# Sums of a closing layer norm moved into the last product, and filler multiplications on TensorE while it waits

## What is computed

```
def second_block(x, ...):
    h = _layernorm(x, ln_in_g, ln_in_b)                        # m = 0
    for layer in range(DEPTH):                                 # DEPTH = 2
        proj = jnp.einsum('bsd,de->bse', h, w_in[layer])
        ...
        y = jnp.einsum('bse,ed->bsd', jnp.concatenate([ya, yb, yc], axis=-1), w_out[layer])
        h = _layernorm(DEEPNORM_ALPHA * h + y, ln_g[layer], ln_b[layer])   # m = 1, 2
    return h

def _layernorm(t, g, b):
    mu = jnp.mean(tf, -1, keepdims=True)
    var = jnp.mean(jnp.square(tf - mu), -1, keepdims=True)
    out = (tf - mu) * lax.rsqrt(var + LN_EPS) * g + b
```

## Time and profile before

| | value |
|---|---|
| median of 3 runs | 1873.46 us |
| profiled execution, time | 1874.83 us |
| profiled execution, span | 1873.0 us |
| mean granted TensorE clock | 0.987 of full speed |
| PE busy (matmuls) | 1822.2 us, 97% |
| DVE / ACT / POOL busy | 1039.5 / 835.8 / 197.8 us |

### The profile page before, as it was taken

How to read it: one execution, slowest core, us unless ns; L and a number is a source line. 1 busy time by engine, 2 the same in 40 slices (tenths; PEclk the granted TensorE clock), 3 DMA queues, 4 the chain that set the end, 5 groups by cost and what they waited for, 6 DMA issues and landing times.

```text
span 1873.0 us, 24302 instructions
## 1 busy us (share of the span) xinstructions
PE 1822.2 (97%) x8918; PEld 1409.8 (75%) x8918; DVE 1039.5 (55%) x1619; ACT 835.8 (45%) x1401; POOL 197.8 (11%) x263
## 2 busy tenths in 40 slices
PE   9899999999999999999999999989999989999997
PEld 5787878888887766677888888868666767866675
DVE  8694454444434767755444434475565476555647
ACT  5233344443323667644444422233466633255753
POOL 7960000000000000000000000033000112200000
PEclk9799999999999999999999999999999999999999
DMA  6332223323333110122223233323111122311111
GB/s 219 76 75 68 90 91 101 96 94 98 93 93 109 47 33 30 57 72 90 96 94 101 91 93 98 101 83 98 62 51 57 46 84 93 98 54 56 57 44 58
DMA packets 58763, 152.20 MB, mean 81 GB/s; under 512 B 17152, under 2 KB 22048, under 8 KB 58672
## 3 DMA queue, kind: packets, MB, share of 16 engines
q1 hardware_dynamic: 52880, 146.43, 24.6%
q0 software_dynamic: 3552, 2.70, 0.5%
q10 hardware_dynamic: 2240, 1.84, 0.4%
HBM read 143.79 MB, written 4.19 MB: 79 GB/s over the span
## 4 chain that ended last, share of the span: by engine, by line
PE 90%; DVE 4%; ACT 3%; issue 1%; DMA 1%; ACTq 1%; SPq 0%; POOL 0%; DVEq 0%
PE bank L1969 19%; PE bank L1970 18%; PE bank L1971 18%; PE bank L2460 3%; PE bank L2462 3%; PE bank L2461 3%; PE bank L2437 2%; PE bank L2423 2%; PE bank L2425 2%; PE bank L2424 2%; PE bank L2192 1%; PE bank L2220 1%; PE bank L2547 1%; DVE wl L1203 1%; PE bank L2475 1%
## 5 line engine op out<-in xcount | busy, mean ns | idle before, releaser
L1203 DVE TENSOR_TENSOR wl<-raw,wh 128x1024 fp32r<-128x1024 f32 (+3 forms) x280 | 323.8, 1157 | 493.5 <-ACT wh L640 490.4
L640 ACT ACTIVATE wh<-raw 128x1024 fp32r<-128x1024 f32 (+3 forms) x280 | 279.1, 997 | 579.8 <-PE bank L1971 504.8
L1969 PE MATMUL bank<-xH,wh 128*128 128x512 f32 x904 | 354.7, 392 | 3.3 <-DVE xL L1209 1.8
L1971 PE MATMUL bank<-xH,wl 128*128 128x512 f32 x904 | 352.1, 389 | 0.0
L1970 PE MATMUL bank<-xL,wh 128*128 128x512 f32 x904 | 352.0, 389 | 0.0
L1969 PEld LDWEIGHTS bank<-xH,wh 128*128 128x128 f32 x904 | 170.0, 188 | 42.6 <-DVE xL L1209 3.1
L1970 PEld LDWEIGHTS bank<-xL,wh 128*128 128x128 f32 x904 | 170.0, 188 | 35.9 <-issue 1.0
L1971 PEld LDWEIGHTS bank<-xH,wl 128*128 128x128 f32 x904 | 169.8, 188 | 35.5
L1969 PE MATMUL bank<-hidH,wh 128*128 128x512 f32 x352 | 137.3, 390 | 0.0
L1971 PE MATMUL bank<-hidH,wl 128*128 128x512 f32 x352 | 136.9, 389 | 0.0
L1970 PE MATMUL bank<-hidL,wh 128*128 128x512 f32 x352 | 136.9, 389 | 0.0
(11 more groups left out here) (445 smaller groups left out, 3325.1 us busy)
## 6 DMA issues: line engine op xcount, KB each, us to landing
raw<-w_gu_dram SPq DMA_DIRECT2D x88, 512.0 KB, 3.3
raw<-w_p_dram SPq DMA_DIRECT2D x64, 512.0 KB, 3.4
raw<-w_dn_dram SPq DMA_DIRECT2D x32, 448.0 KB, 3.3
raw<-w_glu_dram SPq DMA_DIRECT2D x16, 512.0 KB, 3.4
raw<-w_dn_dram SPq DMA_DIRECT2D x16, 512.0 KB, 3.5
raw<-w_out_dram SPq DMA_DIRECT2D x16, 512.0 KB, 3.3
raw<-w_in_dram SPq DMA_DIRECT2D x8, 512.0 KB, 7.9
raw<-w_o_dram SPq DMA_DIRECT2D x8, 512.0 KB, 3.3
```

Of the source, the lines that this page charges most:

```text
L640: nc.scalar.activation(wh[:, (st.base + u) % 2, 0:kts * P], raw[:, (st.base + u) % 4, 0:kts * P], ACT.Copy).then_inc(w_high, 1)
L1203: nc.vector.tensor_tensor(wl[:, s, 0:kts * P], raw[:, (st.base + u) % 4, 0:kts * P], wh[:, s, 0:kts * P].bitcast(F32), ALU.subtract).then_ ...
L1969: nc.tensor.matmul(bank, wh[:, s, w], hi[:, k, :], start=first and kt == 0, stop=False)
L1971: ins = nc.tensor.matmul(bank, wl[:, s, w], hi[:, k, :], start=False, stop=last and kt == kts - 1)
```

## The change

The two sums that are known before the last tile (L2376 and L2379 of before) leave `layer_norm` and become `known_sums(m)`, which is called inside the last product of dn1, out0 and out1, with the hook `between` that `product` already has: ahead of tile 5 of the last (seven-tile) block of dn1, ahead of tile 6 of the last (eight-tile) block of out0 and out1. With them goes the wait for `ln_sum`. What stays in `layer_norm` is L2378, L2381 and their waits. Behind these, for m = 0 and 1, come 18 new matmuls of 512 columns, minus_unit by the high part of qk's first weight block, into bank 5, whose contents nobody reads. Ahead of them is a wait for the split of that block.

```diff
+            def known_sums(m):
+                pe.wait_ge(sem("ln_sum"), 2 * m + 2)
+                nc.tensor.matmul(banks[7][:, :], const("ones"), acc[:, :], start=True, stop=False)
+                nc.tensor.matmul(banks[6][:, :], const("ones"), square_sum, start=True, stop=False)
+
             def feed_forward(layer, n, h):
...
-                        product(st, i, u, hidH, hidL, banks[tile % 4][:, :], first=u % 3 == 0, last=u % 3 == 2)
+                        product(st, i, u, hidH, hidL, banks[tile % 4][:, :], first=u % 3 == 0, last=u % 3 == 2,
+                                between=(5, lambda: known_sums(0)) if layer and i and u == st.n - 1 else None)
...
             def layer_norm(m):
-                pe.wait_ge(sem("ln_sum"), 2 * m + 2)
-                nc.tensor.matmul(banks[7][:, :], const("ones"), acc[:, :], start=True, stop=False)
                 pe.wait_ge(sem("ln_centred"), 8 * m + 8)
                 nc.tensor.matmul(banks[7][:, :], const("ones"), xT[:, KD - 1, :], start=False, stop=True).then_inc(sem("ln_delta"), 1)
-                nc.tensor.matmul(banks[6][:, :], const("ones"), square_sum, start=True, stop=False)
                 pe.wait_ge(sem("ln_sq"), 8 * m + 8)
                 nc.tensor.matmul(banks[6][:, :], const("ones"), squares[3], start=False, stop=True).then_inc(sem("ln_stat"), 1)
+                if m < 2:
+                    st = stages[f"qk{m}"]
+                    pe.wait_ge(w_split, st.base + 5)
+                    for _ in range(18):
+                        nc.tensor.matmul(banks[5][:, :], minus_unit[:, :], wh[:, st.base % 2, 0:S], start=True, stop=True)
...
-                    product(st, u // 4, u % 4, gH, gL, out_bank(layer, u))
+                    product(st, u // 4, u % 4, gH, gL, out_bank(layer, u),
+                            between=(6, lambda: known_sums(layer + 1)) if u == KD - 1 else None)
```

## The result

The kernel after takes 1878.92 us (median of 20 runs, 1875.69 to 1881.42), the kernel before 1875.1 us in the 20 runs beside them. The ratio is 1.0019, with a 95% interval from 1.0013 to 1.0026: slower by 2.4 to 4.9 us, 3.6 at the ratio itself. The profiled execution took 1879.28 us.

A forecast was written before the change was run, and what follows sets the result against it. TensorE, busy for 97% of the span, was taken as the bound. 5.16 + 0.7 - 2.8 = +3.1 us gave 1877.9 on the profiled execution, 1877.4 from the median 1873.46; forecast 1877.5 us, range 1874.9 to 1880.2.

The forecast's parts named there:

- Part 1: In the closings, taking out the known sums gains nothing, since they ran in idle holes or beside other work.
- Part 2: In the dense last products, four fp32 passes cost 1.72 us each, 5.16 us for three closings.
- Part 3: In norm 1's last product, TensorE now waits for ln_sum: cost 0.7 us, bounds 0.55 and 0.8.
- Part 4: Behind closings 0 and 1, the filler holds the clock at full for qk's first products: gain 2.8 us.
- B: Clock falls all the same in or behind the new idle spell, filler gains nothing: 1879.3 us, up to 1880.5; chance 0.14.
- C: Chain view is right, each closing gets 0.86 us shorter: change +0.5 us, 1874.0 to 1875.3 us; chance 0.10.
- D: Sums find cover in the last product's slack, only the clock's gain is left: 1870.7 us; chance 0.04.

The follow-up runs named there:

- e3: Kernel after with level 1 on VectorE moved behind the variance; one execution took 1879.64 us.
- e4: Kernel before with level 1 on VectorE moved behind the variance; one execution took 1877.4 us.
- e8: Kernel after with only the sum of acc moved into the last product, the square sum back in the closing; one execution took 1873.27 us.
- e1: Kernel after without the 18 filler matmuls, only the known sums moved; ratio 1.0035 to the kernel before.
- e5: Kernel after with the known sums of norms 1 and 2 ahead of tile 7 instead of tile 6; one execution took 1878.63 us.
- e9: Kernel before with 12 filler matmuls added; ratio 0.9997 to the kernel before.
- e2: Kernel before with the 18 filler matmuls added and nothing else; ratio 0.9983 to the kernel before.
- e6: Kernel before with 6 filler matmuls added; ratio 1.0000 to the kernel before.
- e10: Kernel before with the 18 filler matmuls, run a second time; ratio 0.9991 to the kernel before.

## Why the prediction was right, step by step

**Part 1, nothing gained by leaving the closing: right.** 0.05 us from L1748 to the next matmul and 1.20 to 1.21 us from level 0 to the variance, before and after. e3 and e4 show what holds the variance, e8 shows that the square sum's place in the closing was free. The chain of waits had charged 0.86 us to L2376: a chain names what ran last, not what would have been late without it.

**Part 2, 1.72 us for each last product: right, 1.75 measured.** The timeline of after has L1970 at 1217.35 where it would have been due at 1215.63. e1 shows the cost by itself; e8 halves it. The 0.03 us above lies behind L1970 (1.36 us from there to L1748, against 1.34 in before, and rounding); no run was made for it.

**Part 3, 0.7 us at norm 1: right, 0.77 (2.52 - 1.75), and 0.70 by e5.** I had the stand as 0.65 us and the restart as up to 0.1; the trace has 0.51 us of idle in the records. By starts it is 0.66: L1971 at 1536.52, the next matmul due 0.23 later at 1536.75, L2164 at 1537.41. The record of the matmul before it covers the difference.

**Part 4, the filler: right in its effect, 1.41 and 1.36 us where I had 1.47 and 1.35.** Tile 3's start is where the gain ends, as worked out: L2405 at 1231.82 takes 0.50 us, behind VectorE's L1777, as the first one behind the idle spell takes 0.47 and those in the row 0.39 or 0.40. It starts 13.11 us behind the last L1748, where the prediction has 13.10 (1228.83 - 1215.73). From there to the next product it is 7.05 us, against 6.90 in before: the second restart cost 0.15 where I had 0.1. What I had too comfortable was the margin. I read rows 6 as a clock that needs more than 2 us of idle; 12 fillers show it fall 2.0 us behind the last record, and the kernel after stands at 1.7. The distance is also no constant. In the twelve traces of this study the clock falls 20 times in an idle spell behind a closing (read from the granted clock in stretches of 0.5 us), between 2.0 and 5.4 us behind TensorE's last record: 2.2, 2.1 and 5.4 us in before, and 5.2, 3.2 and 4.7 us in e1. So three falls were too few to read a margin from, and that 1.7 us sufficed is in part luck. One reading of rows 6 was off too: 0.83 in 1866 to 1867 puts the third fall at 1866.66, which is 5.4 us and not 5.5 behind 1861.30. Its clock held in all six closings of the three traces with that spell (after, e3, e5). Whether it ever falls there in an execution that was not profiled stays open.

The Trainium skill's page TensorE: Matmul & The Clock Gate, section Why this matters for your kernels, warns of idle gaps over about 3 us. e9's trace disagrees: 2.24 us of idle already cost most of the gain there.

**The sum.** 1.75 + 2.52 + 1.75 - 1.41 - 1.36 = 3.25 us by the stretches in front of norm 2's tail, where 3.1 was forecast for these executions; by ratio 3.6, with 2.4 to 4.9 as its interval. The difference of the two medians is 3.8, and the forecast had 4.0 (1877.5 less 1873.46). The 1878.92 itself is 1.4 above the 1877.5 because the 20 runs of the kernel before have 1875.1 as their median, where the three at first had 1873.46. e1 and e2 take the change apart: +6.6 for the sums and -3.2 for the filler give 3.4. The argument that slow stretches differ from one execution to the next, and with them the gain, holds as well: e1 has one of 2.8 us and one of 4.2. The ten slow first products in the traces of before, e1, e4, e6 and e9 give its price: from 2.8 to 5.8 us of slow work the stretch behind the last L1748 goes from 20.98 to 22.33 us, 0.46 us for each, and with the clock full it is 20.1. So 2.8 us of slow work leave 0.9 us to gain, and two such closings 1.8, where the prediction has 1.9 for 3 us each. The forecast lay at the bound of 0.2%, and so does the result. Rivals B and C fell; of D, cover inside the last product, nothing was seen. Two small slips in the prediction's sums change nothing here: the range has 1874.9 and 1880.2 for what rivals C and B have as 1875.3 and 1880.5, and the parts of C and D beyond -0.2% add up to 0.07, not 0.06.

## What to carry to other kernels

Before work is moved from a wait into a dense stretch, ask in the timeline whether it was in the wait's way: an engine's idle hole is the cheapest place for it, and a product at full pace the dearest. When an engine queue is what holds an instruction, an earlier input gives nothing until the queue's order changes, and then only if nothing else holds what comes next: in e3 the variance came 0.47 us sooner and the first low part not at all. A filler that keeps TensorE's clock up is worth about half of the slow stretch less what the next engine then holds back; its length has to be fitted from the trace at both ends, since here 12 were too few in the one trace taken, 18 held the clock in every trace, and 36 were worse than none. The filler alone (e2) is what was worth having.

## What the runs showed of the hardware

The clock can fall after work has begun again: with 6 fillers, 3.60 us of idle, it fell 0.53 us into the product. Idle spells of 0.8 and of 1.7 us were harmless in all twelve closings that have them (after, e2, e3, e5, e8, e10), those of 2.24 us were not, and closing 2 of before kept the clock for 5.4 us behind the last record.

The first L1772 of a closing is longer than the others. L1772's minimum is 0.73 us and the first takes 0.98 in e1, while POOL's L576 still runs beside it. The first pair of L1772 ends with POOL and not with its own start, as the rows of four traces show (norm 0, in us behind the last L1748):

| | first L1772 | POOL's L576 done | pair of L1772 takes | pair ends behind POOL | first L1777 |
|---|---|---|---|---|---|
| e4 | 6.03 | 6.32 | 1.50 | 1.21 | 7.66 |
| before | 5.87 | 6.30 | 1.65 | 1.22 | 7.65 |
| after | 5.88 | 6.40 | 1.72 | 1.20 | 7.73 |
| e3 | 5.67 | 6.39 | 1.93 | 1.21 | 7.74 |

The profile's times of POOL are rough, but in all 24 closings of norms 0 and 1 in the twelve traces the pair ends 1.20 to 1.22 us behind POOL. It would explain why the variance, moved by up to 0.47 us, moved no L1777. With 12, 18 or 36 fillers POOL is done some 0.08 us later, and so is the product's first matmul, so the filler is not quite free. That POOL is the cause was not tried: no run takes L576 away from the first L1772.
